# One f32 transpose of the normalised tile of x, split into f16 halves on the way out of PSUM

## The chip, the cores and the metric

The kernel runs on one core of a Trainium2 chip. It is a single launch, and the metric is device time in microseconds (us), from the first instruction to the last. Four compute engines work side by side, each on its own list of instructions: TensorE (PE, with the loading of its stationary operand as PEld), VectorE (DVE), ScalarE (ACT) and GpSimd (POOL). SyncE (SP) issues the transfers. They meet through semaphores alone: an instruction waits until a counter has reached a value, and counts another one up when it is done.

## What is computed

One residual layer: RMSNorm of x, one wide projection, two groups of heads (a gated delta rule over chunks, and sliding-window attention with sinks), an output projection and a second RMSNorm.

```python
h = rmsnorm(x, pre_norm_w[l])                       # x: (1, 4096, 1024) f32
proj = jnp.einsum('bsd,de->bse', h, w_in[l])        # 3336 columns
(qa, ka, va, za, ba, aa, qb, kb, vb, zb) = jnp.split(proj, IN_OFFSETS, axis=-1)
qkv = silu(causal_depthwise_conv(concat([qa, ka, va]), conv_w[l]))
o_a = rmsnorm(gated_deltanet(qkv...), dn_out_norm_w[l]) * silu(za)
o_b = sliding_window_sink_attention(rope(qb), rope(kb), vb, sinks) * silu(zb)
y = jnp.einsum('bse,ed->bsd', concat([o_a, o_b]), w_out[l])
x = x + rmsnorm(y, post_norm_w[l])
```

The change touches the first line only: how the normalised x reaches the projection. The matrix product needs x with its 1024 features on the partitions, so each tile is transposed; and it is done in f16 with both operands split into a high half and a low half (high = the value rounded to f16, low = the rest), three products for one.

## The kernel before

**Tiles and steps.** The 4096 rows are 32 tiles of 128. Every engine's function has a `step(t, p, mix, proj, prep)`; `proj` is the projection of tile t, `mix` the head groups and the output projection of tile m = t - 1, `prep` the making ready of tile t + 1. Steps 0 and 1 are written out, steps 2 to 29 are a hardware loop whose body is two steps (`run_steps`, 14 rounds), steps 30 to 32 are written out again. So 13 of the passages from one step to the next go through the loop's branch. The order within an engine is written by hand. On TensorE the pieces of the projection (`fill`, L379 and L386) are put between the small dependent products of the head groups, to cover their waits.

**x.** In step t, ScalarE's `normalise(t + 1)` (L598, L600) squares x for its sum and then writes x times its scale as f16 into `x_half[:, 0]`, the high half. VectorE's `low_half` (L784) makes the low half from x in f32 and the high half. At the step's end TensorE's `turn_x` (L357) transposes both halves, 8 blocks of 128x128 each, as f16 into PSUM banks 6 and 7 (`x_turned`). VectorE's `copy_xt` (L792) copies the two banks into `xt_half` (`xt_ready`). The scratch tile `shared` holds `x_half`, and at other times the softmax, the rotary input and the result of `finish`.

**What stands around it on VectorE, in its order:** L784 `low_half`; L840 the gate; L1093 (waits for TensorE's transposes L578); L834 a SiLU; L1098 the low half of group A's output, which waits for ScalarE's high half L744; L792 `copy_xt`; then the last convolution (`convolve(FILL_Q)`, L823 and L825), whose input ScalarE fills (`conv_fill`, L619 to L622), and its SiLU (L834) behind ScalarE's tanh (L629). With that the step is over. The next one begins with L920, L922, L924, four L927, and `finish(m - 1)` (L1112, twice), which reads the output projection out of banks 4 and 5 and counts up `y_used`; it waits for `y_rs`, which comes from ScalarE's squares (L753, behind the tanh on ScalarE) by way of three small POOL operations.

**On TensorE** the same passage is: L578, 48 products of `fill`, `turn_x`, the output projection L564, then in the next step L441 to L455, 72 products of `fill(3)`, and `per_head(4, k4, k4)` (L394), which overwrites bank 4 and so waits for `y_used`.

Setup: VectorE takes the maxima of eight pieces of w_in as they land (L1121), with tile 0's `low_half` and `copy_xt` ahead of the fourth; nothing of the projection starts before these maxima have set the scale of the weights.

Of the kernel before, what the change touches and what calls it, by code (L numbers as in the profile page):

```python
# [25 lines left out]
ALU = mybir.AluOpType  # L26
ACT = mybir.ActivationFunctionType
# [47 lines left out]
def build(nc, x, pre_norm_w, w_in, conv_w, dn_a_log, dn_dt_bias, dn_out_norm_w, sw_sinks, w_out,  # L75
# [8 lines left out]
    with ExitStack() as ctx:  # L84
# [26 lines left out]
        soft = shared[:, :].rearrange("p (h n) -> p h n", n=128)  # L111
        x_half = shared[:, :].bitcast(F16).rearrange("p (s n) -> p s n", s=2)
        rot_in = shared[:, 0:512].rearrange("p (h n) -> p h n", h=8)
# [47 lines left out]
        def cut(at, n):  # L161
# [35 lines left out]
            sem(n) for n in ("setup_link", "neg_a_exp", "pool_set", "post_w_ready"))  # L197
        x_sq_ready, x_rs_ready, xh_ready, xl_ready, x_turned, xt_ready = (
            sem(n) for n in ("x_sq_ready", "x_rs_ready", "xh_ready", "xl_ready", "x_turned", "xt_ready"))
        fill_ready = sems("fill_ready", 7)  # L200
# [91 lines left out]
        def _(sp):  # L292
# [27 lines left out]
            def step(t, p, mix, proj, prep):  # L320
                m = t - 1
                if prep:
                    done(sp, xl_ready, t)
                    sp.dma_start(x_in[:, :], x[0, bass.ds((t + 1) * TOK, TOK), :]).then_inc(x_loaded, 16)
                if proj:
                    done(sp, q_rot_ready, m)
                    sp.dma_start(rot_tab[:, :], rotary[bass.ds(t * TOK, TOK), :]).then_inc(rot_loaded, 16)
                if mix:
                    if isinstance(m, int) and m == 0:
                        sp.wait_ge(wo_ready, 1)  # L330
                    else:
                        sp.wait_ge(stored, m * 16)
                    sp.dma_start(y_out[:, :], x[0, bass.ds(m * TOK, TOK), :]).then_inc(res_loaded, 16)
                    done(sp, post_ready, m)
                    sp.dma_start(out[0, bass.ds(m * TOK, TOK), :], y_out[:, :]).then_inc(stored, 16)
# [6 lines left out]
        def _(pe):  # L342
# [4 lines left out]
            def turn_x(n):  # L347

                done(pe, xh_ready, n)
                done(pe, w_ready, n - 2)  # L350
                done(pe, o_ready, n - 2)
                for s in range(2):
                    if s:
                        done(pe, xl_ready, n)
                    dst = bank[6 + s][:, :].bitcast(F16).rearrange("p (c n) -> p c n", c=NC)
                    for c in range(NC):
                        last = nc.tensor.transpose(dst[:, c, :], x_half[:, s, 128 * c:128 * c + 128], ident16)  # L357
                last.then_inc(x_turned, 1)
# [233 lines left out]
        def _(act):  # L592
# [3 lines left out]
            def normalise(n):  # L596
                act.wait_ge(x_loaded, (n + 1) * 16)
                f(x_half[:, 0, :], x_in[:, :], ACT.Square, accum_out=x_sq).then_inc(x_sq_ready, 1)  # L598
                done(act, x_rs_ready, n)
                f(x_half[:, 0, :], x_in[:, :], ACT.Identity, scale=x_rs).then_inc(xh_ready, 1)  # L600

# [53 lines left out]
            def step(t, p, mix, proj, prep):  # L655
# [86 lines left out]
                if mix:  # L742
                    done(act, out_a_raw, m)
                    f(out_a_half[:, 0, :, :], heads(3), ACT.Copy).then_inc(out_a_high, 1)  # L744
                if proj:
                    conv_fill(t, p, FILL_Q)
                    conv_tanh(t, 0)
                    if not mix:
                        w_out_high(3)
# [6 lines left out]

            normalise(0)

            act.wait_ge(w_scale_ready, 1)
# [12 lines left out]
        def _(dve):  # L772
# [8 lines left out]
            v.tensor_scalar(sinks8, sinks8, DH_B ** 0.5, None, ALU.mult)  # L781
            def low_half(n):
                done(dve, xh_ready, n)
                v.scalar_tensor_tensor(x_half[:, 1, :], x_in[:, :], x_rs, x_half[:, 0, :], ALU.mult,  # L784
                                       ALU.subtract).then_inc(xl_ready, 1)

            def copy_xt(n, last_fill):
                done(dve, x_turned, n)
                if last_fill:
                    done(dve, fill_ready[FILL_Q], n - 1)  # L790
                for s in range(2):
                    last = v.tensor_copy(xt_half[:, s, :, :].rearrange("p c n -> p (c n)"),  # L792
                                         bank[6 + s][:, :].bitcast(F16))
                last.then_inc(xt_ready, 1)
# [101 lines left out]
            def step(t, p, mix, proj, prep):  # L896
# [186 lines left out]
                if proj:  # L1083
                    convolve(t, FILL_K, [3])
                if prep:
                    low_half(t + 1)
                if proj:
# [12 lines left out]
                if prep:  # L1100
                    copy_xt(t + 1, True)
                if proj:
# [13 lines left out]
            for c in range(NC):  # L1116
                dve.wait_ge(w_loaded[c], 64)
                if c == 3:
                    low_half(0)
                    copy_xt(0, False)  # L1120
                last = v.tensor_reduce(w_max[:, c:c + 1], w_raw[:, c + 1, :], AX_X, ALU.max,  # L1121
                                       apply_absolute_value=True)
# [205 lines left out]
```

## Time and profile before

| | us |
|---|---|
| median of 3 runs | 2563.4 |
| lowest, highest | 2559.67, 2566.13 |
| span of the profiled execution | 2562.6 |
| TensorE busy | 2370.1 (92%) |
| VectorE busy | 1646.1 (64%) |
| ScalarE busy | 746.6 (29%) |
| mean granted TensorE clock | 0.987 |

The profile is of one execution; its span is 0.8 us under the median of the runs. A step takes some 74 us where it stays in the loop's body. Busy shares are averages: the work is one chain of steps, and what counts in each is which engine comes last at the few places where TensorE waits.

### The profile page before, as it was taken

To read this page: it belongs to the slowest core of one execution; us is meant where nothing else is said; L and a number is where in the kernel's file an instruction comes from. 1 tells how busy PE (TensorE), PEld (TensorE's weight loads), DVE (VectorE), ACT (ScalarE), POOL (GpSimd) and SP (SyncE) were. 2 spreads that over 40 slices of the span, in tenths; PEclk is the share of its full clock that TensorE was granted. 3 is DMA by queue.
4 is the path that set the end of the run, shared out by engine and by line. 5 is a ranking of instruction groups with operands and counts; after the bars stand their busy time and mean duration, and the time that the engine had idled before them with its cause. 6 is when DMAs were issued, how large, how long until landed. Compare 5 with 4: busy or idle time off the path is not lost.

```text
span 2562.6 us, 65999 instructions
## 1 busy us (share of the span) xinstructions
PE 2370.1 (92%) x27393; PEld 2055.3 (80%) x27393; DVE 1646.1 (64%) x4489; ACT 746.6 (29%) x1816; POOL 573.2 (22%) x746
## 2 busy tenths in 40 slices
PE   0589999999999999999999999999999999999996
PEld 0488888888887888888888888888888788788875
DVE  5876656666666665666666666666666666666663
ACT  1532323222232232223232232322233223233221
POOL 0112222222222222222222122222222222222221
PEclk9999999999999999999999999999999999999997
DMA  7000000000000000000000000000000000000000
GB/s 294 19 19 27 28 28 1 27 28 27 28 27 2 27 27 27 27 28 20 9 28 27 28 27 27 2 27 28 27 28 27 3 27 27 28 27 27 19 2 25
DMA packets 26366, 75.81 MB, mean 30 GB/s; under 512 B 5129, under 2 KB 9538, under 8 KB 25026
## 3 DMA queue, kind: packets, MB, share of 16 engines
q1 hardware_dynamic: 26050, 71.29, 8.0%
q8 instruction: 236, 3.87, 0.6%
q14 instruction: 80, 0.66, 0.1%
HBM read 54.50 MB, written 16.78 MB: 28 GB/s over the span
## 4 chain that ended last, share of the span: by engine, by line
PE 80%; DVE 11%; issue 6%; ACT 2%; DMA 1%; SPq 0%; DVEq 0%; POOLq 0%; POOL 0%; ACTq 0%
PE bank L379 28%; PE bank L401 11%; PE bank L564 10%; PE bank L386 10%; PE bank L394 8%; DVE qkv L825 4%; PE bank L418 2%; PE bank L532 2%; PE bank L498 2%; DVE w_raw L1162 1%; PE bank L357 1%; PE bank L519 1%; ACT inv_u L661 1%; PE bank L412 1%; DVE small L864 1%
## 5 line engine op out<-in xcount | busy, mean ns | idle before, releaser
L379 PE MATMUL bank<-xt_half,w_raw 128*128 128x128 f16 x15360 | 936.6, 220 | 54.4 <-DVE w_raw L1162 53.9
L379 PEld LDWEIGHTS bank<-xt_half,w_raw 128*128 128x128 f16 x15360 | 900.8, 99 | 61.1 <-DVE w_raw L1162 54.1
L825 DVE SCALAR_TENSOR_TENSOR qkv<-conv_in,cols,qkv 128x128 f32<-128x128 f32 x1152 | 409.9, 398 | 3.5
L386 PE MATMUL bank<-w_raw,xt_half 128*128 128x264 f16 (+1 forms) x1536 | 282.9, 328 | 0.0
L661 ACT ACTIVATE inv_u<-bank 128x512 f32<-128x512 f32 x160 | 95.0, 594 | 457.9 <-PE bank L418 457.9
L386 PEld LDWEIGHTS bank<-w_raw,xt_half 128*128 128x128 f16 x1536 | 148.8, 101 | 76.8 <-issue 5.3
L401 PEld LDWEIGHTS bank<-prod,inv_u 128*128 128x128 f32 x1280 | 161.5, 193 | 47.5 <-DVE prod L907 36.9
L401 PE MATMUL bank<-prod,inv_u 128*128 128x64 f32 x1280 | 165.8, 272 | 32.9 <-ACT inv_u L661 32.1
L913 DVE TENSOR_TENSOR inv_t<-inv_t,bank 128x256 f32<-128x256 f32 x160 | 67.4, 421 | 190.8 <-PE bank L401 190.8
L1222 POOL TENSOR_TENSOR shared<-shared,small 128x1024 f32<-128x1024 f32 x32 | 60.8, 1899 | 571.7 <-DVE small L1015 571.7
L401 PEld LDWEIGHTS bank<-inv_t,mt 128*128 128x128 f32 x1280 | 161.1, 192 | 17.2 <-issue 5.7
L564 PE MATMUL bank<-w_o,inv_t 128*128 128x512 f16 x768 | 172.7, 382 | 2.2 <-DVE inv_t L1098 2.2
L564 PE MATMUL bank<-w_o,out_b_half 128*128 128x512 f16 x768 | 171.0, 379 | 0.0
L629 ACT ACTIVATE tanh_c<-qkv 128x512 f32<-128x512 f32 x96 | 60.4, 630 | 377.8 <-DVE qkv L825 377.8
L401 PE MATMUL bank<-inv_t,mt 128*128 128x64 f32 x1280 | 166.6, 273 | 1.7 <-DVE inv_t L913 1.7
L907 DVE TENSOR_TENSOR prod<-bank,masks 128x256 f32<-128x256 f32 x160 | 67.2, 420 | 140.7 <-PE bank L401 140.7
L564 PEld LDWEIGHTS bank<-w_o,inv_t 128*128 128x128 f16 x768 | 74.2, 98 | 86.7 <-DVE inv_t L1098 2.4
L564 PEld LDWEIGHTS bank<-w_o,out_b_half 128*128 128x128 f16 x768 | 73.8, 98 | 83.1
L840 DVE SCALAR_TENSOR_TENSOR w_raw<-tanh_z,bank 128x512 f32<-128x512 f32 x64 | 43.7, 683 | 121.1 <-ACT tanh_z L638 121.1
L394 PE MATMUL bank<-qkv 128*128 128x128 f32 x512 | 73.8, 304 | 44.1 <-DVE shared L1112 44.1
L394 PEld LDWEIGHTS bank<-qkv 128*128 128x128 f32 x512 | 67.8, 213 | 46.6 <-DVE shared L1112 46.6
L1255 POOL TENSOR_TENSOR small<-small 128x1 f32<-128x1 f32 x32 | 6.2, 193 | 429.8 <-ACT prod L753 429.8
(204 smaller groups left out, 3665.8 us busy)
## 6 DMA issues: line engine op xcount, KB each, us to landing
x_in<-in_x_dram SPq DMA_DIRECT2D x32, 512.0 KB, 3.8
y_out<-in_x_dram SPq DMA_DIRECT2D x32, 512.0 KB, 3.8
out_dram<-y_out SPq DMA_DIRECT2D x32, 512.0 KB, 2.9
w_raw<-in_w_in_dram SPq DMA_DIRECT2D x8, 1024.0 KB, 12.5
w_o<-in_w_out_dram SPq DMA_DIRECT2D x8, 512.0 KB, 13.0
w_raw<-in_w_in_dram SPq DMA_DIRECT2D x8, 384.0 KB, 11.4
w_raw<-in_w_in_dram SPq DMA_DIRECT2D x8, 256.0 KB, 12.5
rot_tab<-in_rotary_dram SPq DMA_DIRECT2D x32, 64.0 KB, 3.4
```

The lines of the kernel that those rows point to most:

```text
L379: last = mm(dst[:, 128 * b:128 * b + 128], w_half[:, c, ws, col:col + 128], xt_half[:, xs, c, :], start=(c == 0 and ws + xs == 0), stop=(c ...
L386: last = mm(dst[:, 0:n_col], xt_half[:, xs, c, :], w_half[:, c, ws, col:col + n_col], start=(c == 0 and ws + xs == 0), stop=(c == NC - 1 a ...
L394: last = mm(bank[b][:, 128 * h:128 * h + 128], lhs[:, h, :], right[:, h, :] if len(right.shape) == 3 else right, start=start, stop=stop)
L401: last = mm(bank[b][0:parts, at + 64 * h:at + 64 * h + 64], lhs[:, h, 0:parts], right[:, h, :, :], start=True, stop=True)
L418: last = nc.tensor.transpose(heads(3)[:, h, :], inv_t[:, h, :], ident)
L564: last = mm(bank[4 + n][:, :], src[:, xs, i, :], w_out_half(c)[:, ws, 512 * n:512 * n + 512], start=(begin and i == 0 and xs + ws == 0), s ...
L629: f(tanh_c[:, :], qkv[:, 4 * g:4 * g + 4, :].rearrange("p h n -> p (h n)"), ACT.Tanh, scale=0.5).then_inc(tanh_c_ready[g], 1)
L661: f(inv_u[:, :, :], heads(3), ACT.Copy).then_inc(u_ready[lv].sem, 1)
L825: last = v.scalar_tensor_tensor(dst, conv_in[:, b, i:i + TOK], tap, dst, ALU.mult, ALU.add)
L907: v.tensor_tensor(halves(prod[:, :, :], lv, 0), packed(2, 0, lv), mask_halves(masks[:, lv, :], lv, 0), ALU.mult).then_inc(p_ready[lv].sem, 1)
L913: v.tensor_tensor(dst, dst, packed(2, 256, lv), ALU.subtract).then_inc(t_ready[lv].sem, 1)
L1222: g.tensor_tensor(soft[:, :, :], soft[:, :, :], bc(row_sum, 128), ALU.mult).then_inc(soft_ready, 1)
```

## The change

`x_half` goes. ScalarE writes the normalised tile in f32 (`x_norm`, all of `shared`), TensorE transposes it once as f32 (8 transposes in place of 16, into the same banks, four to a bank). Then ScalarE copies both banks to f16, which is the high half (`xt_high_half`, two instructions, new), and VectorE subtracts that from the banks, which is the low half (`xt_low_half`, two instructions in place of `copy_xt`'s two). `low_half` goes, with its wait on TensorE (`xl_ready`).

```diff
-                done(pe, xh_ready, n)
+                done(pe, x_norm_ready, n)
                 done(pe, w_ready, n - 2)
                 done(pe, o_ready, n - 2)
-                for s in range(2):
-                    if s:
-                        done(pe, xl_ready, n)
-                    dst = bank[6 + s][:, :].bitcast(F16).rearrange("p (c n) -> p c n", c=NC)
-                    for c in range(NC):
-                        last = nc.tensor.transpose(dst[:, c, :], x_half[:, s, 128 * c:128 * c + 128], ident16)
+                for c in range(NC):
+                    last = nc.tensor.transpose(heads(6 + c // 4)[:, c % 4, :], x_norm[:, 128 * c:128 * c + 128], ident)
                 last.then_inc(x_turned, 1)
...
-                f(x_half[:, 0, :], x_in[:, :], ACT.Identity, scale=x_rs).then_inc(xh_ready, 1)
+                f(x_norm, x_in[:, :], ACT.Identity, scale=x_rs).then_inc(x_norm_ready, 1)
+
+            def xt_high_half(n, last_fill):
+                done(act, x_turned, n)
+                if last_fill:
+                    done(act, fill_ready[FILL_Q], n - 1)
+                for s in range(2):
+                    last = f(xt_half[:, 0, 4 * s:4 * s + 4, :], heads(6 + s), ACT.Copy)
+                last.then_inc(xt_high, 1)
...
                     f(out_a_half[:, 0, :, :], heads(3), ACT.Copy).then_inc(out_a_high, 1)
+                if prep:
+                    xt_high_half(t + 1, True)
                 if proj:
                     conv_fill(t, p, FILL_Q)
...
-            def low_half(n):
-                done(dve, xh_ready, n)
-                v.scalar_tensor_tensor(x_half[:, 1, :], x_in[:, :], x_rs, x_half[:, 0, :], ALU.mult,
-                                       ALU.subtract).then_inc(xl_ready, 1)
-
-            def copy_xt(n, last_fill):
-                done(dve, x_turned, n)
-                if last_fill:
-                    done(dve, fill_ready[FILL_Q], n - 1)
+            def xt_low_half(n):
+                done(dve, xt_high, n)
                 for s in range(2):
-                    last = v.tensor_copy(xt_half[:, s, :, :].rearrange("p c n -> p (c n)"),
-                                         bank[6 + s][:, :].bitcast(F16))
+                    last = v.tensor_tensor(xt_half[:, 1, 4 * s:4 * s + 4, :], heads(6 + s),
+                                           xt_half[:, 0, 4 * s:4 * s + 4, :], ALU.subtract)
                 last.then_inc(xt_ready, 1)
...
                 if c == 3:
-                    low_half(0)
-                    copy_xt(0, False)
+                    xt_low_half(0)
```

On VectorE, in the second half of the loop's body, from the last gate to the last convolution, before (`bank` are the PSUM banks, `w_raw` here the gate's buffer, `inv_t` group A's output halves):

```order
L784 SCALAR_TENSOR_TENSOR shared<-x_in,small,shared 128x1024 [waits xh_ready]
L840 SCALAR_TENSOR_TENSOR w_raw<-tanh_z,bank 128x512 [waits tanh_zb_ready]
L1093 TENSOR_TENSOR bank<-bank,w_raw 128x512 [waits o_turned]
L834 SCALAR_TENSOR_TENSOR qkv<-tanh_c,qkv 128x512 [waits tanh_c_ready1]
L1098 TENSOR_TENSOR inv_t<-bank,inv_t 128x512 [waits out_a_high]
L792 COPY xt_half<-bank 128x1024 [waits fill_ready6,x_turned]
L792 COPY xt_half<-bank 128x1024
L823 TENSOR_SCALAR qkv<-conv_in,cols 128x128 [waits qs_ready,conv_in_ready0]
```

and now:

```order
L840 SCALAR_TENSOR_TENSOR w_raw<-tanh_z,bank 128x512 [waits tanh_zb_ready]
L1091 TENSOR_TENSOR bank<-bank,w_raw 128x512 [waits o_turned]
L834 SCALAR_TENSOR_TENSOR qkv<-tanh_c,qkv 128x512 [waits tanh_c_ready1]
L1096 TENSOR_TENSOR inv_t<-bank,inv_t 128x512 [waits out_a_high]
L72 REGISTER_ALU
L792 TENSOR_TENSOR xt_half<-bank,xt_half 128x512 [waits xt_high]
L792 TENSOR_TENSOR xt_half<-bank,xt_half 128x512
L823 TENSOR_SCALAR qkv<-conv_in,cols 128x128 [waits qs_ready,conv_in_ready0]
```

The instruction ahead of the gate is gone, and L792 waits for ScalarE and no longer for TensorE. On ScalarE, at the same place, before:

```order
L744 ACTIVATE inv_t<-bank 128x512 [waits out_a_raw]
L619 ACTIVATE conv_in<-halo 128x4x3 [waits conv_in_ready0,conv_ready1,fill_ready6]
L620 ACTIVATE conv_in<-bank 128x4x128
L70 REGISTER_ALU
L622 ACTIVATE halo<-bank 128x12 [waits halo_used]
L629 ACTIVATE tanh_c<-qkv 128x512 [waits qkv_ready1,conv_ready0]
```

and now:

```order
L748 ACTIVATE inv_t<-bank 128x512 [waits out_a_raw]
L603 ACTIVATE xt_half<-bank 128x512 [waits fill_ready6,x_turned]
L603 ACTIVATE xt_half<-bank 128x512
L623 ACTIVATE conv_in<-halo 128x4x3 [waits conv_in_ready0,conv_ready1,fill_ready6]
L624 ACTIVATE conv_in<-bank 128x4x128
L70 REGISTER_ALU
L626 ACTIVATE halo<-bank 128x12 [waits halo_used]
L633 ACTIVATE tanh_c<-qkv 128x512 [waits qkv_ready1,conv_ready0]
```

The two new copies stand ahead of the filling of the convolution's input. The head of the loop's body on VectorE keeps its order; these rows are of before, and `finish` is L1110 in the changed kernel:

```order
L283 UNCONDITIONAL_BRANCH
L283 ISA
L72 REGISTER_ALU [waits g_row_t]
L920 COPY small<-bank 128x4 [waits exp_cols_ready]
L922 COPY small<-bank 128x4 [waits g_col_t]
L924 TENSOR_TENSOR small<-small 128x4 [waits g_cols_used]
L927 SCALAR_TENSOR_TENSOR decay<-bank,small,c 128x128 [waits aw_ready]
L927 SCALAR_TENSOR_TENSOR decay<-bank,small,c 128x128 x3
L1112 SCALAR_TENSOR_TENSOR shared<-bank,small,w_raw 128x512 [waits y_rs_ready]
```

What moves is where this head lies in VectorE's program: counting every instruction, waits that stand alone among them, 318 stood ahead of the loop's body and 313 do now; the body had 382 and has 378.

## Rows read from the trace of the kernel before

**Rows 1.** The page's first part: busy us (share of the span) xinstructions.
```profile
PE 2370.1 (92%) x27393; PEld 2055.3 (80%) x27393; DVE 1646.1 (64%) x4489; ACT 746.6 (29%) x1816; POOL 573.2 (22%) x746
```
**Rows 2.** TensorE's waits from 95 us on: us in total, times, longest.
```profile
PE bank L394 <- DVE shared L1112: 44.1, 14, 3.5
...
PE bank L451 <- DVE xt_half L792: 4.5, 1, 4.5
```
**Rows 3.** Chain that ended last, inside the body: start us, us, what.
```profile
1046.36 0.89 PE bank L357 x16
...
1054.38 4.02 PE bank L379 x72
```
**Rows 4.** Timeline of VectorE, inside the body: start, us, what [idle before <-releaser].
```profile
1055.92 1.41 DVE L1112 SCALAR_TENSOR_TENSOR shared<-bank,small,w_raw 128x512 f32<-128x512 f32 x2 [0.27 <-POOL small L1259]
```
**Rows 5.** Timeline of VectorE across the loop's branch.
```profile
1121.16 1.29 DVE L792 COPY xt_half<-bank 128x1024 f16<-128x1024 f16 x2 [1.52 <-PE bank L357]
1122.37 0.86 DVE L823 TENSOR_SCALAR qkv<-conv_in,cols 128x128 f32<-128x128 f32 x4
...
1130.49 0.16 DVE L920 COPY small<-bank 128x4 f32<-128x4 f32 x1 [2.35 <-issue]
1132.85 0.16 DVE L922 COPY small<-bank 128x4 f32<-128x4 f32 x1 [2.19 <-issue]
...
1134.17 1.40 DVE L1112 SCALAR_TENSOR_TENSOR shared<-bank,small,w_raw 128x512 f32<-128x512 f32 x2
```
**Rows 6.** Timeline of TensorE across the loop's branch.
```profile
1135.62 2.78 PE L394 MATMUL bank<-qkv 128*128 128x128 f32 x16 [3.17 <-DVE shared L1112]
```
**Rows 7.** Timeline of ScalarE across the loop's branch.
```profile
1120.27 0.21 ACT L619 ACTIVATE conv_in<-halo 128x12 f32<-128x12 f32 x1 [1.35 <-PE bank L379]
...
1121.00 0.18 ACT L622 ACTIVATE halo<-bank 128x12 f32<-128x12 f32 x1
```
**Rows 8.** Nearest kin of the new work: chain, timelines, and L519's weight loads.
```profile
1082.66 0.87 PE bank L519 x8
...
1083.57 0.60 ACT L706 ACTIVATE shared<-bank 128x512 f32<-128x512 f32 x1 [0.28 <-PE bank L519]
1084.07 0.59 ACT L707 ACTIVATE shared<-bank 128x512 f32<-128x512 f32 x1
...
1072.95 1.28 DVE L998 TENSOR_TENSOR shared<-bank,small 128x512 f32<-128x512 f32 x2
...
L519 PEld LDWEIGHTS bank<-c,shared x256: 139/141/146, 172.0 to 2515.5; 128*128 128x128 f32 x128
```
**Rows 9.** Instruction queues: packets, MB, share; the page, then 1128:1134, then 1183:1184.5.
```profile
q14 instruction: 80, 0.66, 0.1%
...
q14 instruction: 3, 0.02, 1.6%
...
q14 instruction: 1, 0.01, 1.9%
```
**Rows 10.** Timeline of VectorE in that last stretch.
```profile
1183.17 0.15 DVE L881 SCALAR_TENSOR_TENSOR small<-small 128x4 f32<-128x4 f32 x1
```
**Rows 11.** Windows behind three branches: us, PE busy, granted clock, DMA share, GB/s.
```profile
373.00:379.00 6.00, 5.95 (x35) 0.50 0.44 147
...
678.00:684.00 6.00, 5.65 (x51) 0.72 0.36 121
831.00:837.00 6.00, 5.55 (x73) 1.00 0.37 129
```
**Rows 12.** Timeline of VectorE in setup.
```profile
37.18 1.28 DVE L784 SCALAR_TENSOR_TENSOR shared<-x_in,small,shared 128x1024 f16<-128x1024 f32 x1 [0.44 <-DMA w_raw<-in_w_in_dram]
39.59 1.29 DVE L792 COPY xt_half<-bank 128x1024 f16<-128x1024 f16 x2 [1.13 <-PE bank L357]
40.80 17.75 DVE L1121 TENSOR_REDUCE small<-w_raw 128x1 f32<-128x3336 f32 x5
```
**Rows 13.** Chain that ended last, in step 0.
```profile
131.57 1.20 DVE shared L784
```

More of the change, by code:

```diff
@@ L111, in build @@
         soft = shared[:, :].rearrange("p (h n) -> p h n", n=128)
-        x_half = shared[:, :].bitcast(F16).rearrange("p (s n) -> p s n", s=2)
+        x_norm = shared[:, :]
         rot_in = shared[:, 0:512].rearrange("p (h n) -> p h n", h=8)
@@ L197, in build @@
             sem(n) for n in ("setup_link", "neg_a_exp", "pool_set", "post_w_ready"))
-        x_sq_ready, x_rs_ready, xh_ready, xl_ready, x_turned, xt_ready = (
-            sem(n) for n in ("x_sq_ready", "x_rs_ready", "xh_ready", "xl_ready", "x_turned", "xt_ready"))
+        x_sq_ready, x_rs_ready, x_norm_ready, x_turned, xt_high, xt_ready = (
+            sem(n) for n in ("x_sq_ready", "x_rs_ready", "x_norm_ready", "x_turned", "xt_high", "xt_ready"))
         fill_ready = sems("fill_ready", 7)
@@ L322, in step @@
                 if prep:
-                    done(sp, xl_ready, t)
+                    done(sp, x_norm_ready, t)
                     sp.dma_start(x_in[:, :], x[0, bass.ds((t + 1) * TOK, TOK), :]).then_inc(x_loaded, 16)
@@ L597, in normalise @@
                 act.wait_ge(x_loaded, (n + 1) * 16)
-                f(x_half[:, 0, :], x_in[:, :], ACT.Square, accum_out=x_sq).then_inc(x_sq_ready, 1)
+                f(x_norm, x_in[:, :], ACT.Square, accum_out=x_sq).then_inc(x_sq_ready, 1)
                 done(act, x_rs_ready, n)
-                f(x_half[:, 0, :], x_in[:, :], ACT.Identity, scale=x_rs).then_inc(xh_ready, 1)
+                f(x_norm, x_in[:, :], ACT.Identity, scale=x_rs).then_inc(x_norm_ready, 1)
[6 more added lines that the diff above has]
+                last.then_inc(xt_high, 1)
             def w_out_high(part):
@@ L757, in _ @@
             normalise(0)
+            xt_high_half(0, False)
             act.wait_ge(w_scale_ready, 1)
@@ L1084, in step @@
                     convolve(t, FILL_K, [3])
-                if prep:
-                    low_half(t + 1)
                 if proj:
@@ L1100, in step @@
                 if prep:
-                    copy_xt(t + 1, True)
+                    xt_low_half(t + 1)
                 if proj:
```

## The prediction

> **What bounds the kernel now.** I read the page first: TensorE is busy for 92% of the span, VectorE for 64% [rows 1]. So only what TensorE does, or what it waits for, can move the time. Then its waits behind setup: the largest is L394 waiting for VectorE's `finish` (L1112), 44.1 us in 14 places, and there is one wait of 4.5 us for `xt_half` [rows 2]. The timelines show where these are. There are two kinds of passage between steps. Inside the loop's body TensorE's 72 products end at 1054.38 + 4.02 = 1058.40 [rows 3] and L394 follows without a wait; L1112 had ended at 1055.92 + 1.41 = 1057.33 [rows 4], so VectorE was ahead by 1.0 us. Across the loop's branch VectorE loses 2.35 us before L920 and 2.19 us before L922, both put down to issue, with nothing awaited [rows 5], and TensorE waits 3.17 us for L1112 [rows 6]. There are 13 branches (the 14th wait is in the last step, which follows no `prep`). Each is also a gap in TensorE's work, and behind it the granted clock falls in some rounds to its lower level (1.2 GHz in place of 2.4): in the 6 us behind the gap the mean is 0.72 or 0.50, or stays at 1.00 [rows 11]. Of the 13 gaps, 6 show 0.72, 2 show 0.50 and 5 show 1.00. That is 6 x 6 x 0.28 + 2 x 6 x 0.50 = 16 us of lost clock in all.
>
> So the question is what the change does to the moment at which VectorE ends L1112.
>
> **The transposes.** TensorE loses 16 f16 transposes per tile, 0.89 us as they stand in the chain [rows 3], and gets 8 in f32. The nearest row is L519, eight f32 transposes of the same tile `shared`: 0.87 us [rows 8]. I take 0 for this term. The bounds are these two rows: a gain of 0.02 x 32 = 0.6 us, and, if the stationary side of the new ones should show as it does for L519 (141 ns each [rows 8]), 8 x 0.141 = 1.13 us, which would be 0.24 x 32 = 8 us of loss. L519 itself goes at 0.87 with those same loads, so the first bound is the likelier by far.
>
> The Trainium skill has a rule that speaks against the change here: its page "TensorE: Matmul & The Clock Gate", section "Weight-path perf modes", says that the fast loading of weights is not used for FP32. The loads of L519 are longer than those of the f16 transposes in this trace too, but at half as many transposes the rows give a draw.
>
> **The hop over ScalarE.** Before, VectorE's two copies start 0.03 us behind the last transpose [rows 5] and take 1.21 us up to the convolution's first instruction (1121.16 to 1122.37). Now ScalarE goes first: two copies of 128x512 out of PSUM take 1.09 us together (1083.57 to 1084.66 [rows 8]), and the handing over some 0.02 more. Then VectorE's two subtractions: L998 is the same shape with a PSUM source, 1.28 us for two [rows 8], as much as the copies' 1.29 [rows 5]. So VectorE reaches the convolution 1.1 us later, in each of the steps with `prep`. Bounds 1.0 and 1.3.
>
> Does ScalarE delay it further? Its `conv_fill` (L619 to L622) takes 0.91 us (1120.27 to 1121.18 [rows 7]) and now stands behind the copies: it ends at 1122.25 + 0.95 = 1123.2, and VectorE wants it at 1122.37 + 1.1 = 1123.5. No wait is added, with 0.3 us in hand. Behind the copies on ScalarE are queued only that, the tanh of this convolution and the squares of y; the tanh waits for VectorE anyway, so the squares, `y_rs` on POOL, and L1112 all shift by the same 1.1 us. `xt_ready` itself comes at 1123.5 and is wanted by TensorE some four microseconds later (it goes through L564 first), so it stays hidden.
>
> **What is removed from VectorE** (L784, 1.28 us) buys nothing in a step of the loop: VectorE then waits 3 us for TensorE before L1093 anyway, and so would 1.28 us more.
>
> **Inside the body** (17 passages without a branch that follow a `prep`): 1.1 us of delay against 1.0 in hand: 0.1 each, 1.7 us. Bounds 0 and 0.3 each, 0 to 5 us.
>
> **Across the branch** the 1.1 us would be paid in full, unless the stall moves, and I think it does. The two idle stretches are fetches of instructions. In the stretch from 1128 to 1134 the queue q14 brings three packets, then none until one between 1183 and 1184.5 [rows 9]. A packet is 0.66 MB / 80 = 8.2 KB. At 1183.2 VectorE executes L881 [rows 10], which in the built program is exactly the 128th instruction behind L922; and at the 256th the next packet comes. So a block is 128 instructions, one boundary lies right between L920 and L922, the branch finds neither of the first two blocks, the second is asked for when the first has come, and arrives 2.36 us behind L920's start (1130.49 to 1132.85 [rows 5]). The change leaves 313 instructions ahead of the body and not 318. If the blocks stay where they are, the boundary falls 5 instructions later in the body: L920, L922, L924 and three of the four L927 are in the first block. They run while the second comes. Then the fourth L927 starts 2.36 us behind L920, and L1112 some 0.27 us behind that, at 2.63, where before it was at 1134.17 - 1130.49 = 3.68 [rows 5]. That is 1.05 us back, against 1.1 lost. I take +0.1 us for each of 13: 1.3 us. The bounds are +1.1 (nothing comes back, 14.3 us) and, if the whole 2.19 us went, 1.1 - 2.2 = -1.1 (14.3 us gained).
>
> **Lost clock.** With the gap at 3.2 to 3.3 us, about as many branches lose clock as now. I take +1 us, one more of the shorter kind on 13 (6 x 0.28 = 1.7 us each), rounded down. Bounds -4 and +5 by two or three rounds more or fewer.
>
> **Setup and step 0.** VectorE has L784, a wait of 1.13 us and the copies from 37.18 to 40.80, then five reductions without a wait until 58.55 [rows 12]. Now only the subtractions stand there, 1.2 us, since everything ahead of them ended long before. 2.4 us are free, but the pieces of w_in land only every 4.1 us, against 3.63 for a reduction: the last would land at about 37.1 + 4 x 4.15 = 53.7, and the last reduction started at 54.9. I take 1.0 us of gain (0.5 to 2.4). In step 0 the chain that ended last goes through L784 itself, 1.20 us [rows 13], then through the scaling of w_out and the copies to TensorE's wait of 4.5 us [rows 2]. It shortens by 1.1 us.
>
> **Sum** against the span: -1.0 - 1.1 + 1.7 + 1.3 + 1.0 + 0 = +1.9, so 2564.5; with the 0.8 us by which the median of the runs is above the span, **2565 us**. Its own range is 2558 to 2575.
>
> **Rivals.**
>
> *The stall does not move* (slower). The blocks are cut from another place, or the second idle stretch is something else than a fetch, tied to L922. Then TensorE's gap grows from 3.2 to 4.3 us at each branch: 14.3 us. A longer gap can only lose more clock: at least the 5 spared ones join, at the 8's mean of 2.0 us, 10 us. Sum -2.1 + 1.7 + 14.3 + 10 = +24: 2587 us. For it: I infer the blocks from packets and positions. Against it: three independent positions fit. It decides over the sign of my result from a remaining delay of about 0.5 us at a branch.
>
> Here the Trainium skill differs from my reading: its page "Runtime: NRT & Kernel Launch", section "Instruction fetch mechanics", has blocks of 16 KiB or 256 instructions, and lets only a taken branch stall, while passing from block to block is mostly hidden. By that rule the idle time before L922 is no fetch and this rival's 2587 us holds. Rows 9 show packets of half that size on q14, and a packet in front of each of the two stretches; I go by them.
>
> *The stall goes altogether* (faster). If the second block is asked for together with the first, or lands before the six instructions are through, L1112 comes 2.2 us earlier than with the stall: 14.3 us gained, and with gaps near 2 us most of the lost clock too, say 10 of 16. Sum -2.1 + 1.7 - 14.3 - 10 = -25: 2539 us. Against it: the second packet came 2.4 us behind the first in this trace, one after the other.
>
> *The f32 transposes show their loads*: +8 us on my forecast, 2573 us. Against it stands L519 as a whole.
>
> *The change is nothing but its savings*: if ScalarE's copies overlap better than L706 and L707 and the slack inside the body holds, 2560 us, no measurable difference.
>
> **How the numbers follow.** Forecast 0.58; stall stays 0.20; loads show 0.05; savings alone 0.10; stall goes 0.07. No change that a measurement can tell is within 0.3%, 7.7 us, of 2563.4: 2555.7 to 2571.1. Faster by more: the last case and a little of the others, 0.09. Slower by more: 0.20, half of 0.05, and 0.08 of the forecast's upper end, 0.31. The same: 0.60. The range goes from 2556 to 2588: it leaves out the faster case and the upper end of the slower one.
>
> **What would show it.** Right: L357's successor at 0.87 us; ScalarE's new copies 1.09 us behind it; the idle time before L922 gone and one of some 1.2 us between two of the L927; TensorE's wait on `finish` at branches 3.2 to 3.4 us; new small waits of 0.1 us inside the body; the first projection 1 us earlier. Wrong: a wait of 4.3 us at branches with the idle time still before L922; or waits of ScalarE's filling in front of the last convolution.

## The result

| | before | changed |
|---|---|---|
| median of 7 runs each, us | 2563.4 | 2572.3 |
| lowest, highest | 2559.67, 2566.13 | 2566.82, 2575.59 |
| span of the profiled execution | 2562.6 | 2569.1 |
| mean granted TensorE clock | 0.987 | 0.986 |

The ratio of the times is 1.0028, with a 95% interval of 1.0018 to 1.0039. The same kernel run again later, in a series of its own (7 runs against 10 of before), gave 1.0042 (1.0026 to 1.0058). By the two ratios the change costs 7 and 11 us, by their intervals together 5 to 15; the medians of the two series differ by 8.9 and 13.7 us. It was forecast at 2565 and lies inside the range of 2556 to 2588, 1.2 us beyond what I had called no change (up to 2571.1).

The page of the changed kernel, its busy line, the answer to [rows 1]:

```profile
PE 2376.0 (92%) x27137; PEld 2057.9 (80%) x27137; DVE 1607.2 (63%) x4457; ACT 777.2 (30%) x1880; POOL 550.3 (21%) x746
```

VectorE has lost 39 us of work, ScalarE gained 31. TensorE issues 256 instructions fewer (8 for 16, in 32 tiles). None of that is the time: TensorE's waits from 95 us on are, the answer to [rows 2] (us in total, times, longest):

```profile
PE bank L390 <- DVE shared L1110: 45.6, 14, 3.7
...
PE bank L447 <- DVE xt_half L792: 4.2, 1, 4.2
```

L390 is L394 of before and L1110 is `finish`. One of the 14 waits, 2.7 us, is the last step's. The 13 at the branches are 42.9 us together, 3.30 each, where before they were 41.4 us, 3.18 each. A look at the branch that [rows 5 to 7] show, now on ScalarE, VectorE and TensorE (start, us, what, idle before):

```profile
1120.13 1.04 PE L353 MATMUL bank<-c,shared 128*128 128x128 f32 x8
1121.21 1.09 ACT L603 ACTIVATE xt_half<-bank 128x512 f16<-128x512 f32 x2 [2.23 <-PE bank L353]
1122.33 1.29 DVE L792 TENSOR_TENSOR xt_half<-bank,xt_half 128x512 f16<-128x512 f32 x2 [2.62 <-ACT xt_half L603]
...
1131.88 0.16 DVE L920 COPY small<-bank 128x4 f32<-128x4 f32 x1 [2.58 <-issue]
1131.96 0.15 DVE L922 COPY small<-bank 128x4 f32<-128x4 f32 x1
1132.15 0.16 DVE L924 TENSOR_TENSOR small<-small 128x4 f32<-128x4 f32 x1
1132.23 0.86 DVE L927 SCALAR_TENSOR_TENSOR decay<-bank,small,c 128x128 f32<-128x128 f32 x3
1134.09 0.35 DVE L927 SCALAR_TENSOR_TENSOR decay<-bank,small,c 128x128 f32<-128x128 f32 x1 [1.00 <-issue]
1134.36 1.40 DVE L1110 SCALAR_TENSOR_TENSOR shared<-bank,small,w_raw 128x512 f32<-128x512 f32 x2
...
1135.81 3.29 PE L390 MATMUL bank<-qkv 128*128 128x128 f32 x16 [3.50 <-DVE shared L1110]
```

The second idle stretch of 2.19 us ahead of L922 is gone. In its place stand 1.00 us between the third and the fourth L927, where the prediction had put the boundary. L1110 starts 2.48 us behind L920, not 3.68: 1.2 us are given back, against the 1.1 that the hop over ScalarE takes.

Inside the loop's body there is a wait that was not there before. VectorE's `finish`, and TensorE's 72 products and what follows:

```profile
1056.78 1.41 DVE L1110 SCALAR_TENSOR_TENSOR shared<-bank,small,w_raw 128x512 f32<-128x512 f32 x2 [0.26 <-POOL small L1256]
...
1053.96 4.18 PE L375 MATMUL bank<-xt_half,w_raw 128*128 128x128 f16 x72
1058.24 1.94 PE L390 MATMUL bank<-qkv 128*128 128x128 f32 x15
```

L390 starts 4.28 us behind the start of the products and 0.05 us behind the end of L1110. That is VectorE's end and not TensorE's work. The same two groups in the kernel before, on the timeline:

```profile
1054.21 4.18 PE L379 MATMUL bank<-xt_half,w_raw 128*128 128x128 f16 x72
...
1058.23 2.00 PE L394 MATMUL bank<-qkv 128*128 128x128 f32 x16
```

There it was 4.02 us. The step from transposes to transposes takes 74.17 us in the body where it took 73.87 (the same to 0.01 in all 13 rounds read): 0.26 us in this place, and 0.05 in the 16 products behind it, which run the slower when they were waited for.

The third part is lost clock. As in [rows 11], the 6 us behind each of the 13 gaps were read; two of the 13 in the changed kernel:

```profile
370.00:376.00 6.00, 6.00 (x46) 5.94 (x46) 5.73 (x14) 0.60 (x1) 3.03 (x2) 0.57 0.52 183
525.00:531.00 6.00, 6.00 (x66) 5.94 (x65) 5.76 (x14) 0.60 (x1) 2.72 (x2) 0.72 0.59 195
```

11 of 13 stand below 1.00, where it had been 8. Taking (1 - granted clock) x 6 us for each, the sum is 18.8 us; the same sum for before is 15.2. These stretches begin at a whole microsecond and cut off the end of the longest slow ones: counted from the end of each gap for as long as the clock stays low, it is 19.9 and 15.9, the numbers that the expectations below use.

Setup: VectorE's reductions of the weights, the answer to [rows 12]:

```profile
36.32 1.29 DVE L792 TENSOR_TENSOR xt_half<-bank,xt_half 128x512 f16<-128x512 f32 x2 [0.40 <-DMA w_raw<-in_w_in_dram]
37.52 10.89 DVE L1118 TENSOR_REDUCE small<-w_raw 128x1 f32<-128x3336 f32 x3
49.05 3.63 DVE L1118 TENSOR_REDUCE small<-w_raw 128x1 f32<-128x3336 f32 x1 [0.63 <-DMA w_raw<-in_w_in_dram]
53.27 3.63 DVE L1118 TENSOR_REDUCE small<-w_raw 128x1 f32<-128x3336 f32 x1 [0.59 <-DMA w_raw<-in_w_in_dram]
```

They now wait for the transfers again, and end at 56.90 where it was 58.55. The first of the eight had started 0.87 us earlier in this execution (22.61 against 23.48), which is the transfer's doing (23.05 and 23.22 in a second trace of each kernel), so 0.8 us are the change's.

### The profile page after: what moved, and what is told of

It is laid out like the page before. It is cut to its first block, busy times and chain, and to the rows that moved or that the text cites. A ratio compares the mean times of both kernels' runs of the same rounds, so it can differ in the third digit from the quotient of the medians.

```text
span 2569.1 us, 65519 instructions
## 1 busy us (share of the span) xinstructions
PE 2376.0 (92%) x27137; PEld 2057.9 (80%) x27137; DVE 1607.2 (63%) x4457; ACT 777.2 (30%) x1880; POOL 550.3 (21%) x746
## 4 chain that ended last, share of the span: by engine, by line
PE 66%; issue 15%; DVE 12%; ACT 3%; POOL 2%; DMA 1%; SPq 1%; POOLq 0%; DVEq 0%; ACTq 0%
PE bank L375 22%; PE bank L397 11%; PE bank L382 10%; PE bank L390 9%; DVE qkv L825 4%; PE bank L560 4%; PE bank L414 2%; PE bank L528 2%; PE bank L494 2%; DVE shared L1110 2%; DVE w_raw L1159 1%; PE bank L515 1%; SPq L309 1%; ACT inv_u L665 1%; PE bank L408 1%
## 5 line engine op out<-in xcount | busy, mean ns | idle before, releaser
L397 PE MATMUL bank<-prod,inv_u 128*128 128x64 f32 x1280 | 165.8, 272 | 32.8 <-ACT inv_u L665 32.0
L390 PE MATMUL bank<-qkv 128*128 128x128 f32 x512 | 78.7, 317 | 47.3 <-DVE shared L1110 45.6
L390 PEld LDWEIGHTS bank<-qkv 128*128 128x128 f32 x512 | 71.7, 224 | 52.8 <-DVE shared L1110 52.8
```

The source lines that it names most:

```text
L390: last = mm(bank[b][:, 128 * h:128 * h + 128], lhs[:, h, :], right[:, h, :] if len(right.shape) == 3 else right, start=start, stop=stop)
L397: last = mm(bank[b][0:parts, at + 64 * h:at + 64 * h + 64], lhs[:, h, 0:parts], right[:, h, :, :], start=True, stop=True)
```

## Experiments

The theory: (1) the hop over ScalarE delays `finish` by 1.1 us in each step; (2) what this costs inside the body is the part of it that exceeds what VectorE had in hand; (3) at the branch VectorE waits for blocks of 128 instructions, and the change has moved a boundary in its favour. The rivals: the time is lost on TensorE, by the f32 transposes; the idle time behind the branch has nothing to do with where the instructions lie.

Point 3 is tested by fillers: VectorE fills one column of an unused buffer, so many times, in setup, where it waits for the weights anyway. They do nothing but push the loop's body back in VectorE's program. For the changed kernel with 8 of them:

```diff
+        filler = sb("filler", [128, 32])
...
             v.memset(halo[:, :, :], 0.0)
+            for i in range(8):
+                v.memset(filler[:, i:i + 1], 0.0)
```

**Five fillers in the changed kernel**: the body begins where it began before the change.

> The changed kernel with 5 one-column fills of an unused buffer put into VectorE's setup, so that again 318 instructions stand ahead of the loop's body on VectorE, as in the kernel before. Theory (the idle time behind the branch is a fetch, and its place goes by the instruction's place in VectorE's program): the second idle stretch is back between L920 and L922 with some 2.2 us, the one ahead of the fourth L927 is gone, finish ends 1.05 us later behind the branch, TensorE waits 4.3 to 4.5 us at branches; 13 x 1.05 = 14 us more, and 5 to 10 us of lost clock more: 2586 to 2596. Rival (the idle time has nothing to do with the place): the same time as the changed kernel, 2572.

Measured: 2594.4 us (2594.05 to 2595.16). VectorE at a branch, and TensorE's wait in total:

```profile
1141.46 0.16 DVE L923 COPY small<-bank 128x4 f32<-128x4 f32 x1 [2.62 <-issue]
1143.94 0.16 DVE L925 COPY small<-bank 128x4 f32<-128x4 f32 x1 [2.31 <-issue]
```

and of its waits

```profile
PE bank L391 <- DVE shared L1113: 60.2, 14, 4.8
```

The idle stretch is back between the same two instructions (L923 and L925 are L920 and L922). The 13 waits are 57.5 us, 4.42 each: 14.6 us more than in the changed kernel. All 13 branches lose clock, 26.0 us by the sum above, 7.2 more. 14.6 + 7.2 = 21.8, and 22.1 were measured between the medians, 23.3 between the two profiled spans. This is the change without the move of the boundary: 1.0118 times the kernel before (1.0101 to 1.0135). So the place in the program does it, and the rival is refuted. It is also what the prediction had called "the stall does not move", at 2587; that was 7 us too low.

**Eight fillers in the changed kernel, three in the kernel before**: both bodies begin at 321.

> The changed kernel with 8 such fills: 321 instructions ahead, so that the loop's body begins exactly where I place a block's beginning, and its 378 instructions lie in three blocks of 128. Theory: the branch waits for one block only, the next arrives while its 128 instructions run. The idle time between the first instructions and finish (1.0 us) goes, TensorE waits 2.3 to 2.5 us at branches, the granted clock falls at few of them: 13 x 1.0 + some 15 of lost clock = 28 us less than the changed kernel, 2544. Should the engine even hold the three blocks of the loop, the idle time behind the branch goes altogether: some 43 us of waits and 20 us of clock, 2510. Rival (place does nothing): 2572.

> The kernel before with 3 such fills, so that its loop's body also begins at 321 (382 instructions, still within three blocks). Theory: the 2.19 us ahead of L922 go, TensorE waits 1.0 us at branches in place of 3.2: 13 x 2.19 = 28 us less, and most of the 16 us of lost clock: 2520 to 2525. With the whole loop held: 2505. Rival (place does nothing): 2563. Against the changed kernel with 8 fills it should be some 20 us faster, since there the hop over ScalarE stands in full at the branches.

Measured: 2513.6 us (2506.16 to 2516.45) and 2506.2 us (2503.56 to 2507.29), 0.9792 and 0.9769 times the kernel before. In the changed kernel VectorE now passes from one step to the next without idle time put down to issue, at the branch too. This is one of the 13 branches:

```profile
1106.54 0.69 DVE L837 SCALAR_TENSOR_TENSOR qkv<-tanh_c,qkv 128x512 f32<-128x512 f32 x1 [0.70 <-ACT tanh_c L634]
1107.15 0.15 DVE L923 COPY small<-bank 128x4 f32<-128x4 f32 x1
1107.22 0.15 DVE L925 COPY small<-bank 128x4 f32<-128x4 f32 x1
...
1108.87 1.41 DVE L1113 SCALAR_TENSOR_TENSOR shared<-bank,small,w_raw 128x512 f32<-128x512 f32 x2 [0.27 <-POOL small L1259]
```

Of the changed kernel's waits with 8 fillers, and then of its page (packets, MB, share):

```profile
PE bank L391 <- DVE shared L1113: 2.7, 1, 2.7
```

```profile
q14 instruction: 15, 0.12, 0.0%
```

No idle time ahead of L923 and L925, one wait for `finish` left (the last step's), and 15 packets on the instruction queue q14 in place of 80 [rows 9]. The difference is 65, five for each of 13 branches. So no instructions are fetched at the branch at all: my first expectation, one stall left, was wrong, and the one I had named second held. The three blocks of the loop stay in the engine. Gone are the 13 waits and the lost clock behind them, in before 41.4 + 15.2 = 56.6 us, and 57.2 were measured; in the changed kernel 42.9 + 18.8 = 61.7, and 58.7 were measured. These are medians. The two profiled spans of the changed kernel differ by 54.6 us only: in the trace with 8 fillers the part up to step 3's transposes is 2.0 us longer and the part from step 30's transposes to the end 5.8 us (155.5 for 149.7), of which more below.

**Twelve and twenty fillers in the changed kernel**: is it the beginning of a block, or the number of blocks?

> The changed kernel with 12 fills: 325 instructions ahead, so the loop's body is not at a block's beginning but (325 to 702) still within the same three blocks. If it is the number of blocks that decides: as with 8 fills, 2513, and 15 packets on the instruction queue. If the body has to begin where a block does: one stall of 2.4 us at each branch, 2540 to 2550, and 80 packets.

> The changed kernel with 20 fills: 333 instructions ahead, the body from 333 to 710 touches a fourth block with its last 6 instructions. If three blocks are held and four are not: the stall at the branch is back, some 80 packets; but the second block is wanted only 116 instructions later, so no second idle time: TensorE waits 2.3 to 2.5 us, 13 x 2.4 + 0 to 10 of lost clock above the kernel with 8 fills: 2544 to 2555. If the engine holds more than three blocks: 2513. If only the place of the boundary near the head mattered: also 2544.

Measured: 2506.9 us (2506.59 to 2507.41) with 12, 2545.5 us (2540.32 to 2548.26) with 20. The instruction queue q14, first with 12, then with 20, and VectorE and TensorE at a branch with 20:

```profile
q14 instruction: 16, 0.12, 0.0%
```

```profile
q14 instruction: 80, 0.66, 0.1%
```

```profile
1122.53 0.16 DVE L923 COPY small<-bank 128x4 f32<-128x4 f32 x1 [2.52 <-issue]
1122.61 0.15 DVE L925 COPY small<-bank 128x4 f32<-128x4 f32 x1
...
1123.91 1.40 DVE L1113 SCALAR_TENSOR_TENSOR shared<-bank,small,w_raw 128x512 f32<-128x512 f32 x2
...
1125.37 2.05 PE L391 MATMUL bank<-qkv 128*128 128x128 f32 x16 [2.03 <-DVE shared L1113]
```

A body that need not begin with a block, but touches only three (325 to 702), is held. Six instructions in a fourth bring back five packets and 2.5 us of idle time at each branch; but only one stall, since the second block arrives long before it is wanted. TensorE's 13 waits are 2.1 us each, and 4 of 13 branches lose clock, 6.6 us.

**The two conversions moved back by one piece of work**, on both engines, in the changed kernel:

```diff
+                if proj:
+                    conv_fill(t, p, FILL_Q)
                 if prep:
                     xt_high_half(t + 1, True)
                 if proj:
-                    conv_fill(t, p, FILL_Q)
                     conv_tanh(t, 0)
...
+                if proj:
+                    convolve(t, FILL_Q, [0], qs_ready if mix else None, m)
                 if prep:
                     xt_low_half(t + 1)
                 if proj:
-                    convolve(t, FILL_Q, range(4), qs_ready if mix else None, m)
+                    convolve(t, FILL_Q, [1, 2, 3])
```

> The changed kernel with the two conversions moved back by one piece of work: on ScalarE the filling of the convolution's input (L623 to L626) ahead of the two copies, on VectorE the first group of the last convolution ahead of the two subtractions. The numbers of instructions stay (313 ahead of the body). Theory (the hop of 1.1 us over ScalarE is what delays VectorE): VectorE works for 0.9 us while ScalarE copies, so most of the hop is hidden, 0.9 us per step; inside the body the 0.25 us per step come back (17 x 0.25 = 4 us), at the branches 13 x 0.9 = 12 us and some of the lost clock, 5 to 15 us: 2572 - 21 to 31 = 2541 to 2551. Rival (the time is lost elsewhere, by the transposes or on TensorE): 2570 or more.

Measured: 2544.0 us (2543.21 to 2548.12), 0.9919 times the kernel before (0.9903 to 0.9936). ScalarE and VectorE in the body (L824 is the convolution's first instruction, L793 the subtraction), and TensorE's wait in total:

```profile
1110.27 1.04 PE L353 MATMUL bank<-c,shared 128*128 128x128 f32 x8
1110.47 0.21 ACT L623 ACTIVATE conv_in<-halo 128x12 f32<-128x12 f32 x1 [1.35 <-PE bank L375]
...
1111.36 1.08 ACT L603 ACTIVATE xt_half<-bank 128x512 f16<-128x512 f32 x2
1111.42 0.87 DVE L824 TENSOR_SCALAR qkv<-conv_in,cols 128x128 f32<-128x128 f32 x4 [1.57 <-ACT halo L626]
1112.47 1.29 DVE L793 TENSOR_TENSOR xt_half<-bank,xt_half 128x512 f16<-128x512 f32 x2 [0.18 <-ACT xt_half L603]
```

and of the waits

```profile
PE bank L390 <- DVE shared L1113: 35.5, 14, 2.8
```

VectorE works for 0.87 us while ScalarE copies, and waits 0.18 us more. The 13 waits fall from 42.9 to 32.8 us, the lost clock from 18.8 to 7.7, and the step in the body from 74.17 back to 73.86: 10.1 + 11.1 + 17 x 0.31 = 26.5 us. The medians differ by 28.3 us. The two profiled spans, from which the terms are read, differ by 22.8: in this run's trace the part behind step 30's transposes is 3.5 us longer (153.2 for 149.7), so not all of the 26.5 us came out at the end. The step is what tells: the transposes are as they were in the changed kernel and the step is back where it was before, so they cost nothing, and that rival is out.

**How much VectorE has in hand**: one instruction that nobody waits for, behind the copies of x in the kernel before, whose body still lies in three blocks.

```diff
+        sink = sb("sink", [128, 4])
...
+            for i in range(1):
+                v.memset(sink[:, i:i + 1], 0.0)
...
                 if prep:
                     copy_xt(t + 1, True)
+                    v.tensor_reduce(sink[:, 3:4], w_half[:, 1, 0, 0:512], AX_X, ALU.max)
```

> The kernel before with one VectorE reduction more behind the two copies of each step's x (128x512 f16, nobody waits for its result), and one fill, so that the loop's body (384 instructions, 321 to 704) fills three blocks. It delays VectorE by 0.5 to 0.65 us in each step. TensorE's start of the group behind finish lies 0.91 us behind the end of finish in that kernel, of which 0.05 us is the handing over: 0.85 us are in hand. Theory: no wait appears, the step keeps 73.87 us, the whole is as with 3 fills, 2506. Rival (in hand is less, or a delay of VectorE costs TensorE elsewhere in the step too): a step of 74.0 us or more. Should 384 instructions not be held, the branches' stall is back and only the steps inside the body tell.

> The same with the reduction twice as wide (128x1024 f16), a delay of 1.0 to 1.2 us. Theory: more than the 0.85 in hand; TensorE waits 0.2 to 0.35 us for finish in each step, which takes 74.1 to 74.25 us, and 29 such passages make 6 to 11 us: 2512 to 2517. By the 1.0 us in hand that my prediction read, 0.0 to 0.2 us each: 2506 to 2512.

Measured: 2508.1 us (2503.67, 2512.61) and 2513.1 us (2511.97, 2514.17). The totals are of two runs each and scatter by as much as the question; the steps do not. First the narrow one, two successive tiles, then the wide one:

```profile
1023.10 1.06 PE L358 MATMUL bank<-masks,shared 128*128 128x128 f16 x16
1096.98 1.06 PE L358 MATMUL bank<-masks,shared 128*128 128x128 f16 x16
...
1099.28 0.68 DVE L1105 TENSOR_REDUCE sink<-w_raw 128x1 f32<-128x512 f16 x1
1099.87 0.86 DVE L826 TENSOR_SCALAR qkv<-conv_in,cols 128x128 f32<-128x128 f32 x4
```

```profile
1028.34 1.06 PE L358 MATMUL bank<-masks,shared 128*128 128x128 f16 x16
1102.53 1.06 PE L358 MATMUL bank<-masks,shared 128*128 128x128 f16 x16
...
1104.83 1.21 DVE L1105 TENSOR_REDUCE sink<-w_raw 128x1 f32<-128x1024 f16 x1
1105.95 0.86 DVE L826 TENSOR_SCALAR qkv<-conv_in,cols 128x128 f32<-128x128 f32 x4
```

The narrow one holds VectorE for 0.59 us and the step is 73.88 (median of 26: 73.87), as without it. The wide one holds it for 1.12 us and makes the step 74.19: 0.32 more, 0.27 of wait and the 0.05 behind it. In hand are 1.12 - 0.27 = 0.85 us, and what goes beyond is paid in full. This is also the changed kernel's 0.30, got without its change.

**Both edits together**, with 8 and with 12 fillers.

> Both edits together: the changed kernel with the moved conversions and 8 fills (321 instructions ahead, loop of 378). What the two showed alone: with the loop in three blocks 2513.6, of which 0.30 us per step is the hop over ScalarE in excess of what VectorE has in hand. Theory: the 0.30 us go in each of some 29 steps, 8.7 us: 2505, with the savings of setup and step 0 below the kernel before with 3 fills (2506.2) or level with it. Rival (the 0.30 us is the transposes' or TensorE's own): 2513.

> Both edits, with 12 fills in place of 8. The changed kernel alone went from 2513.6 with 8 fills to 2506.9 with 12, and its steps were the same 74.17 us; the difference stands in the granted clock of the last 70 us. The steps here should take 73.86 us. If the clock at the end is as good as it was with 12 fills: 2506.9 - 27 x 0.3 = 2499; if it is as with 8: 2506.

Measured: 2505.8 us (2503.85 to 2508.53) and 2504.7 us (2500.33 to 2505.72), 0.9767 (0.9744 to 0.979) and 0.9764 (0.9745 to 0.9784) times the kernel before. Inside the body the steps take 73.86 us, as expected, and yet against the 2506.9 of the changed kernel with 12 fillers only 1 to 2 us are left of 9. With 12 fillers both times, two places took the rest. The passages through the branch take 74.12 us in the mean, and not 73.86, which is 3.4 us in 13 passages; in the one looked at (74.34) TensorE's first products behind the branch start 0.5 us late, and TensorE does not wait for `finish` there. (In the changed kernel with 12 fillers a branch costs next to nothing, 74.20 for 74.18.) And the part from step 30's transposes to the end is 5.8 us longer (153.1 for 147.3). In it TensorE waits often. Its clock there, from 2440 to 2500 us, with 8 fillers and with 12 in the changed kernel without the moved conversions:

```profile
2440.00:2500.00 60.00, 48.82 (x281) 40.94 (x280) 26.79 (x65) 12.35 (x31) 9.65 (x11) 0.70 0.05 18
```

```profile
2440.00:2500.00 60.00, 44.93 (x294) 34.25 (x294) 27.19 (x61) 12.61 (x32) 10.38 (x14) 0.86 0.05 18
```

(0.86 - 0.70) x 60 = 10 us between two kernels whose work there is the same. It differs between kernels and, with 8 fillers, between runs (2506.16 and 2516.45). What sets it I have not settled; below some 8 us, totals of these kernels can't be compared by one profile, and the steps have to be. The two with both edits are the fastest kernels of the study, level with the kernel before with three fillers.

**Both kernels a second time**, for the clock.

> The changed kernel itself once more, for a second trace. Its branches in the first trace waited 3.3 us in the mean and 11 of 13 lost clock, where before it was 3.2 us and 8 of 13. If the difference in lost clock (3.9 us) belongs to the change, 10 or more of 13 again and about 20 us; if it is chance between executions, anything from 7 to 12.

> The kernel before itself once more, for a second trace. Its first trace lost 15.9 us of clock behind branches, in 8 of 13; the changed kernel 19.9 and 20.5 us, in 11 and 12 of 13. If the difference belongs to the change: 7 to 9 of 13 again and some 16 us. If it is chance: anything up to 12.

Measured: 2575.2 us in the median of 7 for the changed one (profiled span 2575.0), 2561.4 us in a single run for before (2559.6). TensorE's waits, changed and before:

```profile
PE bank L390 <- DVE shared L1110: 45.4, 14, 3.4
```

```profile
PE bank L394 <- DVE shared L1112: 42.9, 14, 3.4
```

The changed kernel loses clock at 12 of 13 branches (19.4 us), before at 8 of 13 (13.4 us). The first expectation held in both: the difference came again, 3.6 and 6.0 us, some 5. With two traces of each kernel I put it down to the change.

## Why the prediction came out as it did

The sign was right and the places of the main losses were named; two sizes were too small. The account, from the two pairs of traces, beside the terms of the prediction:

| us | forecast | first pair | second pair |
|---|---|---|---|
| up to the first branch, less 3 passages | -2.1 | -4.2 | -0.8 |
| inside the body, 17 passages | +1.7 | +5.1 | +5.1 |
| TensorE's 13 waits at branches | +1.3 | +1.5 | +2.5 |
| lost clock behind them | +1.0 | +3.6 | +6.0 |
| behind the last of the 13 gaps | 0 | 0 | +2.7 |
| sum | +1.9 | +6.0 | +15.5 |
| spans, measured | | +6.5 | +15.4 |

The medians differ by 8.9 us in the first series, where the spans differ by 6.5. I had added 0.8 us to go from the span to the median. Every run whose time and span are both on record is 1.8 to 1.9 us longer than its own span, and which execution was profiled does the rest, so this term rested on one execution's chance.

**The transposes**: right. L353 holds TensorE for 0.88 us, L357 for 0.89, and the loads of the f32 operand don't show.

**The hop over ScalarE**: right, and to a hundredth. From the release of L1091 to the end of `finish` VectorE needs 1.10 us more than before, ScalarE's two copies take 1.09, and its filling of the convolution's input adds no wait.

**The removal of L784**: right; VectorE's wait before L1091 grew from 3.03 to 4.22 us.

**Inside the body**: this is the step that failed. "VectorE was ahead by 1.0 us" is wrong by 0.15, for a plain reason: I took TensorE's end from the chain (1054.38 + 4.02 = 1058.40) and VectorE's end from the timeline (1057.33). A chain gives TensorE's groups by when they hand on, and its pieces begin 0.17 us later than the timeline's. On one and the same view L394 starts at 1058.23, 0.90 us behind VectorE, and 0.05 of this is the handing over. In hand were 0.85 us, as the delays of 0.59 and 1.12 us confirm from outside. 1.10 - 0.85 = 0.25 us of wait, to which come 0.05 in the products behind it. That is 0.30 and not 0.10 for each of 17, 5.1 us and not 1.7. It was the upper bound that the prediction had stated. The term was mis-sized, and the mechanism was right.

**Across the branch**: right in its mechanism and nearly in its size. The boundary moved by the five places to where it was put, and 1.2 us were given back; without this the change is 22 us worse (five fillers). The sentence against the Trainium skill, page "Runtime: NRT & Kernel Launch", section "Instruction fetch mechanics", stands for VectorE's list: with blocks of 256 and crossings hidden, five fillers could not have done this. It holds for q14 alone. The page of the profile has a second instruction queue, q8, that I had not looked at: 3.87 MB in 236 packets in the kernel before, 16.4 KB each, the size that the section gives. Its count did not follow VectorE's fillers (235 or 236 in every run). What that section says of the branch (a target outside the blocks that are held stalls) agrees with the 2.5 us of idle time before the body's first instruction with twenty fillers, and with none in a body that is held.

**Lost clock**: right in its sign, too small, 1.0 for some 5 us. "About as many branches" was the sloppy step. The gaps are 3.2 us before and 3.3 after in the mean, and 8 of 13 branches lost clock at the one (in both traces) and 11 or 12 at the other. The other kernels give a trend of the count: 4 of 13 at 2.1 us, 5 at 2.5, all 13 at 4.4. But the length of a gap does not settle it. In the kernel before, the gap of 3.50 us was followed by the full clock ([rows 11], 831 to 837 us), and one of 3.00 us was not:

```profile
831.45 2.05 PE L394 MATMUL bank<-qkv 128*128 128x128 f32 x16 [3.50 <-DVE shared L1112]
2050.76 3.12 PE L394 MATMUL bank<-qkv 128*128 128x128 f32 x16 [3.00 <-DVE shared L1112]
...
2050.00:2056.00 6.00, 5.24 (x43) 0.72 0.29 103
```

In the changed kernel 2.93 us (at 1442.30) lost clock and 3.18 us (at 1595.67) did not. So a tenth of a microsecond more in the mean gap is not shown to be what costs three branches more. The time from one gap to the next differs between the kernels too (a round without lost clock takes 151.3 us before and 151.7 in the changed kernel), and so may when a gap falls count. No run separates the two: that the loss grew is shown, why it grew is open.

**Setup and step 0**: setup was right, 0.8 us for 1.0. From the first product of the projection to TensorE's first group of L447 step 0 gave 2.2 us in the first pair and 1.2 in the second, for the 1.1 forecast. The rest of the -4.2 is the earlier transfer, 0.87 us, and 0.3 us more. In the second pair some 1.5 us were lost again by the first branch. The granted clock accounts for it: from 135 to 300 us it is 0.98 in the changed kernel and 0.99 in the kernel before, 0.01 x 165 = 1.7 us, while in the first pair both kernels lost the same ahead of the first branch.

The rivals: the stall that does not move, which five fillers brought about, was priced a little low in each term: against the kernel before its waits grew by 16.1 us (57.5 for 41.4) and not 14.3, its lost clock by 10.8 and not 10, and the body's 5.1 us were taken for 1.7. The stall that goes altogether was given 0.07, which was right for this change, but it lay eight instructions away (three in the kernel before) and was worth more than I had written: the changed kernel with 8 fillers is 50 us faster than the kernel before, and not 25, and the kernel before with three is 57 us faster. I had read the second idle stretch as a thing that the change would shift, and had not asked of the first why it was there.

## What to carry to other kernels

Count the instructions of a hardware loop, and where its body begins: here a VectorE body that fits three blocks of 128 runs without fetching. One that spills into a fourth by six instructions stands idle for 2.5 us at each branch, and where a boundary lies a few instructions behind the branch's target it is 3.6 to 4.9 us. Only VectorE's list was tested. Three one-column fills ahead of the loop made the kernel before 2.3% faster, more than the change under study could win or lose. A conversion that is split over two engines is a hop, and is to be put where the receiving engine has other work for as long as the first one takes. And slack is read from one view only: the same clock for both engines, start of the waiting instruction against end of the awaited one.

## What was new about the hardware

- The instruction queue q14 carried 80 packets with a VectorE body that touches four blocks, and 15 or 16 with one that touches three. Nothing showed a middle state.
- Packets differ by queue: 8.2 KB on q14 (0.66 MB in 80), 16.4 KB on q8 (3.87 MB in 236).
- In one and the same trace the granted clock fell behind a gap of TensorE of 3.00 us and did not fall behind one of 3.50 us.
- The block behind the one that the branch waited for came 2.2 to 2.5 us after it: L922 against L920 [rows 5] 2.36, the fourth L927 against L920 in the changed kernel 2.21, L925 against L923 with five fillers 2.48.
- Products that start after a wait of 0.25 us took 1.89 us in place of 1.84.
- Two kernels with the same work from 2440 to 2500 us differed by 10 us there in lost clock alone (0.70 against 0.86).
